# First attention of a two-block transformer kernel: split values stationary, probabilities of two token tiles moving

## The chip, the cores and the metric

The kernel runs on one core of a Trainium2 chip. The metric is the device time of one execution in microseconds (us); the kernel before takes 1032.56 us, the median of 3 runs (1032.04 to 1034.12). A lower time is better.

## The reference

One call computes two transformer blocks over 512 tokens of width 1024, all in fp32. The change concerns the attention of the first block. It has 16 heads of width 64: eight "b" heads (dilated windows, merged into one softmax with a per-distance additive term) and eight "a" heads (each token attends to the 128 keys that an indexer scores highest). Cut to what matters:

```
proj = rms_norm(x) @ w_in                  # q, k, v, z of both kinds of heads, and the indexer
for every head:
    logits = q k^T * scale + bias          # causal; 'a': only the selected keys
    p      = softmax(logits)
    o      = p v
mixed = concat(a_out * silu(za), b_out * silu(zb))
x     = x + mixed @ w_out                  # then block 2: projections, second attention, feed-forward
```

## The kernel before, in words

It is one hand-ordered program: every engine has its own list of instructions, and semaphores (wait_ge, then_inc) tie them together. Sixty-four steps make the first attention; `steps1` lists (tile i, kind, head) in groups of eight: the four token tiles of 128 tokens for the two heads r = 0, 1 of a pair, "b" first, then "a". Step t of token tile i looks at i + 1 blocks of 128 keys. The loop on every engine goes over t by two, so that one iteration has both heads of a pair at one token tile.

Large products are made in three fp32r products of a high and a low part (`three`, L869: high x high, high x low, low x high). The scores are such products (`pair1`, L1020), two heads side by side on the halves of the array. What an iteration does, by engine:

- **TensorE**: waits `l_done` for the last pair's scores to be read, then the scores of t and t + 1; the fillers of this iteration (`fill`, L869: one K chunk of a z projection at a time, 64 chunks in 56 steps, so 2 or 3 chunks of three products of 512 columns); rows of the output projection from step 58 on (`row1`, table ROW_AT); once a pair the transposes of the finished output (`mixed_transposes`, L1047); then for the steps t - 2 and t - 1 the transposes of the probabilities (`turn1`, L1029) and for t - 4 and t - 3 the value products (`value1`, L1039): per block of keys the turned probabilities, fp32, 128x128, are stationary and 64 columns of fp32 values move; the result has tokens on the partitions and collects the eight outputs of a group (both heads, four tiles) in one bank.
- **VectorE**: adds the bias to the scores and takes the row maximum in one instruction (L2164, printed as CUSTOM_DVE_ANT_0 and a read of the accumulator); copies turned probabilities out of PSUM into `probsT1` (L2177; in the second half of the steps the odd ones are ScalarE's, L1682); divides a group by its softmax denominators (`finish1`, L2120 and L2123); multiplies with silu(z) (`mix`, L2132, one operand in PSUM) and takes the low part of the mixed rows (`mixed_low`, L2146); scales the finished z tiles (`gate_rows`, L2139 and L2140); splits weight units (`low`, L1992).
- **ScalarE**: exp with the sum over the row (`exps`, L1505), silu of two z tiles at four places (L1674), the rounding of weight units (`high`, L1540), of mixed rows (L1652) and of output weights (L1669).
- **GpSimd**: from step 34 on adds the selection mask to the bias of the "a" heads (`combo`, L2612).
- **SP** issues the loads: weight units (`load_unit`, L688) into a ring of five raw and four rounded places, strips of the bias (L724, 32 transfers), parts of `w_out`.

```
pe.wait_ge(t_free, TT[("pt", u)] + 1)
for j in range(i + 1):
    last = mm(bank[6 + o % 2][:, at:at + HD], probsT1[u % 2][:, j * P:(j + 1) * P],
              v1["v" + br][:, j, h * HD:(h + 1) * HD], start=(j == 0), stop=(j == i))
```

Behind the loop comes the rest of the first row of the output projection (`first_row`), the other rows (`residual`), and the first transposes of block 2 (`h_transposes`, L918), whose input is the norm of x (L1961). The second attention, from about 513 us on, has its own code, which the change leaves alone: values split into halves that are stationary together (L1273), roundings and differences of turned probabilities (L1784, L2363), low rows (L1791, L2373), reciprocals (L2418) and scaling on GpSimd (L2664) ahead of the transposes (L1259).

## Time and profile before

| | |
|---|---|
| median of 3 runs | 1032.56 us (1032.04 to 1034.12) |
| the profiled execution | 1032.51 us |
| its span | 1030.7 us |
| TensorE busy, matmuls / weight loads | 99% / 82% |
| VectorE busy | 65% |
| ScalarE busy | 52% |
| GpSimd busy | 35% |
| granted TensorE clock, mean | 1.00 |

The span is the profiled part of the execution; 1.8 us lie around it. Busy is the share of the span in which an engine has an instruction under way; matmuls overlap in a pipeline and their ends are modelled, so that a busy TensorE may still wait. The granted clock is given as a share of full speed.

### The profile page before, as it was taken

To read this page: it belongs to the slowest core of one execution; us is meant where nothing else is said; L and a number is where in the kernel's file an instruction comes from. 1 tells how busy PE (TensorE), PEld (TensorE's weight loads), DVE (VectorE), ACT (ScalarE), POOL (GpSimd) and SP (SyncE) were. 2 spreads that over 40 slices of the span, in tenths; PEclk is the share of its full clock that TensorE was granted. 3 is DMA by queue.
4 is the path that set the end of the run, shared out by engine and by line. 5 is a ranking of instruction groups with operands and counts; after the bars stand their busy time and mean duration, and the time that the engine had idled before them with its cause. 6 is when DMAs were issued, how large, how long until landed. Compare 5 with 4: busy or idle time off the path is not lost. (4 is left out here: it accounts for less than half of the span.)

```text
span 1030.7 us, 14348 instructions
## 1 busy us (share of the span) xinstructions
PE 1019.2 (99%) x5310; PEld 843.8 (82%) x5310; DVE 665.9 (65%) x1141; ACT 534.4 (52%) x960; POOL 365.7 (35%) x334
## 2 busy tenths in 40 slices
PE   9999999999999999999999999999999999999997
PEld 7788888888878898988887788889888888888885
DVE  5578998675765346824567779444323325999996
ACT  7454445554673255545567884134434436554554
POOL 0022011003330001910165430007779965874562
PEclk9999999999999999999999999999999999999999
DMA  9655332314420285233200362239999951443552
GB/s 335 119 113 119 88 96 67 82 47 130 144 93 1 78 257 164 62 82 82 54 9 1 109 239 62 82 102 322 347 351 333 352 193 62 152 138 138 204 184 82
DMA packets 99637, 146.24 MB, mean 142 GB/s; under 512 B 6208, under 2 KB 60224, under 8 KB 99568
## 3 DMA queue, kind: packets, MB, share of 16 engines
q1 hardware_dynamic: 86016, 129.70, 38.6%
q10 hardware_dynamic: 12768, 12.88, 3.9%
q0 software_dynamic: 784, 2.75, 1.8%
q8 instruction: 42, 0.69, 0.3%
q14 instruction: 27, 0.22, 0.1%
HBM read 123.69 MB, written 21.63 MB: 141 GB/s over the span
## 5 line engine op out<-in xcount | busy, mean ns | idle before, releaser
L2462 DVE TENSOR_TENSOR w_lo<-wring,w_hi 128x1024 fp32r<-128x1024 f32 x32 | 53.0, 1658 | 105.8 <-ACT w_hi L1846 105.8
L1992 DVE TENSOR_TENSOR u_lo<-wring,u_hi 128x1024 fp32r<-128x1024 f32 (+1 forms) x64 | 80.8, 1272 | 50.9 <-ACT u_hi L1540 50.4
L869 PE MATMUL bank<-u_hi,h_hi 128*128 128x512 f32 (+1 forms) x288 | 111.0, 385 | 0.1
L869 PE MATMUL bank<-u_hi,h_lo 128*128 128x512 f32 (+1 forms) x288 | 109.4, 380 | 0.0
L869 PE MATMUL bank<-u_lo,h_hi 128*128 128x512 f32 (+1 forms) x288 | 109.1, 379 | 0.0
L1540 ACT ACTIVATE u_hi<-wring 128x1024 fp32r<-128x1024 f32 (+1 forms) x64 | 65.8, 1033 | 79.1 <-PE bank L869 57.2
L869 PE MATMUL bank<-h_hi,w_hi 128*128 128x512 f32 (+2 forms) x272 | 103.3, 380 | 0.0
L869 PE MATMUL bank<-h_hi,w_lo 128*128 128x512 f32 (+2 forms) x272 | 103.3, 380 | 0.0
L869 PE MATMUL bank<-h_lo,w_hi 128*128 128x512 f32 (+2 forms) x272 | 103.2, 380 | 0.0
L869 PE MATMUL bank<-h_hi,u_hi 128*128 128x512 f32 x224 | 94.4, 421 | 0.4 <-ACT arena L1482 0.2
L1370 PE MATMUL bank<-s_hi,f_hi 128*128 128x512 f32 x224 | 87.5, 391 | 0.7 <-DVE f_lo L2496 0.7
L869 PE MATMUL bank<-h_hi,u_lo 128*128 128x512 f32 x224 | 87.8, 392 | 0.0
L869 PE MATMUL bank<-h_lo,u_hi 128*128 128x512 f32 x224 | 87.8, 392 | 0.0
L1371 PE MATMUL bank<-s_hi,f_lo 128*128 128x512 f32 x224 | 87.4, 390 | 0.0
L1372 PE MATMUL bank<-s_lo,f_hi 128*128 128x512 f32 x224 | 87.3, 390 | 0.0
L1846 ACT ACTIVATE w_hi<-wring 128x1024 fp32r<-128x1024 f32 x32 | 33.9, 1060 | 91.9 <-PE bank L869 91.9
L2664 POOL TENSOR_SCALAR arena<-arena,stats 128x128 f32<-128x128 f32 (+3 forms) x64 | 40.4, 641 | 95.0 <-DVE stats L2418 94.9
L2488 DVE TENSOR_TENSOR s_lo<-wring,s_hi 128x2048 fp32r<-128x2048 f32 (+1 forms) x32 | 67.8, 2119 | 5.7 <-ACT s_hi L1876 5.6
L869 PEld LDWEIGHTS bank<-u_hi,h_hi 128*128 128x128 f32 x288 | 54.1, 188 | 11.5 <-issue 1.2
L2612 POOL TENSOR_TENSOR junk<-arena,x 128x256 f32<-128x256 f32 (+2 forms) x24 | 24.1, 1025 | 108.8 <-DVE stats L2164 80.3
L869 PEld LDWEIGHTS bank<-u_lo,h_hi 128*128 128x128 f32 x288 | 54.2, 188 | 10.1
L869 PEld LDWEIGHTS bank<-u_hi,h_lo 128*128 128x128 f32 x288 | 54.2, 188 | 9.4
(374 smaller groups left out, 2543.7 us busy)
## 6 DMA issues: line engine op xcount, KB each, us to landing
wring<-in_w_in SPq DMA_DIRECT2D x60, 512.0 KB, 3.9
wring<-in_w_ff ACTq DMA_DIRECT2D x12, 1024.0 KB, 8.2
wring<-sums_kept SPq DMA_DIRECT2D x16, 768.0 KB, 4.2
wring<-in_w_ff SPq DMA_DIRECT2D x22, 512.0 KB, 6.2
wring<-in_w_ff SPq DMA_DIRECT2D x32, 256.0 KB, 3.3
sums_kept<-wring SPq DMA_DIRECT2D x22, 256.0 KB, 4.9
arena<-in_w_out SPq DMA_DIRECT2D x4, 1024.0 KB, 5.1
wring<-in_w_out SPq DMA_DIRECT2D x2, 2048.0 KB, 13.5
```

The costliest lines, as they stand in the source:

```text
L869: last = mm(b, lhs, rhs, start=(start and n == 0), stop=(stop and n == 2))
L1370: mm(b, f[0][:, token], w[0][:, high], start=start, stop=False)
L1371: mm(b, f[1][:, token], w[0][:, high], start=False, stop=False)
L1372: return mm(b, f[0][:, token], w[1][:, lows], start=False, stop=stop)
L1540: run(u_hi[u % HI_UNITS][:, 0:unit_cols(u)], raw_unit(u), ACT.Copy).then_inc(u_hi_done, 1)
L1846: run(dst, src, ACT.Copy).then_inc(w_hi_done, 1)
L1992: v.tensor_tensor(u_lo[u % RAW_UNITS][:, 0:cols], raw_unit(u), u_hi[u % HI_UNITS][:, 0:cols].bitcast(F32), ALU.subtract).then_inc(u_lo_don ...
L2462: v.tensor_tensor(cut(w_lo[ring3(m)]), src, cut(w_hi[ring3(m)]).bitcast(F32), ALU.subtract).then_inc(w_lo_done, 1)
L2488: v.tensor_tensor(s_lo[pair_place(m)][:, at:PAIR], pair_raw(m)[:, at:PAIR], s_hi[m % 4][:, 0:PAIR - at].bitcast(F32), ALU.subtract)
L2612: g.tensor_tensor(combo[c % 2][:, 0:(i + 1) * P], strips[:, h, (NT - 1 - i) * P:S], mask_of[i], ALU.add)\
L2664: g.tensor_scalar(place, place, den2[:, u:u + 1], gates[:, i, at:at + 1], ALU.mult, ALU.mult).then_inc(scaled, 1)
```

## The change

The value products of the first attention take the form of the second attention's:

- Values are evicted twice (`v1_both`: rounded to the high part, and raw; GpSimd's `value_low` makes the low part), so that the high and low parts of one head's 64 columns stand side by side as one stationary operand of 128 columns.
- Turned probabilities are split too: ScalarE rounds (`turned_high`), VectorE takes the difference (`turned_low`), into places (`pt1`) in which the blocks of two token tiles lie next to each other, block j of both tiles in 256 columns. They are the moving operand. The result has the head's columns on the partitions and tokens along the row; rows 64 to 127 hold the product with the low values. `low_rows_of` (ScalarE) and `collect1` (VectorE) add them.
- `value1(o, n, r)` handles token tiles 2n and 2n + 1 of head r of pair o. For n = 0 both heads come at the iteration after the pair's last scores, for n = 1 both heads come together in the iteration t % 8 == 4.
- The probabilities are divided before they are turned: VectorE takes reciprocals of two denominators per iteration, GpSimd multiplies (`scaled`). `finish1` and the transposes of the finished output (`mixed_transposes`) go; `mix` reads the collected output from SBUF.
- Transposes stand two iterations behind the scores instead of one, and logits have eight places instead of four.
- The new operands need space: weight units of z get two raw and two rounded places (`raw_place`, `hi_place`), the strips have room for two pairs and are loaded pair by pair (`load_strips`, 48 transfers; GpSimd's `send_strip` sends four heads instead of eight), the third part of `w_out` lies elsewhere (`late_raw`), and the first units of block 2 load into places that come free with the last value product.
- Tables that set the order (LOW1, GATE_AT, WO_HIGH, ROW_AT) and the end of the loop (the last pair gated in two halves) are written for the new sequence.

```diff
+            def turned_high(u):
+                act.wait_ge(t_full, k + 1)
+                if o >= 1:
+                    act.wait_ge(pv_done, 4 * (o - 1) + 2 * (i // 2) + r + 1)
+                run(turned_place("hi", i, r), bank[4 + k % 2][:, 0:(i + 1) * P].rearrange("p (m s) -> p m s", s=P), ACT.Copy)\
+                    .then_inc(pt_hi_done, 1)
...
-            def value1(u):
-                for j in range(i + 1):
-                    last = mm(bank[6 + o % 2][:, at:at + HD], probsT1[u % 2][:, j * P:(j + 1) * P],
-                              v1["v" + br][:, j, h * HD:(h + 1) * HD], start=(j == 0), stop=(j == i))
...
+            def value1(o, n, r):
+                g, h, q, end = "v" + "ba"[o // 4], 2 * (o % 4) + r, 2 * o + n, 2 * n + 1
+                pe.wait_ge(t_free, TT[("pt", NH * o + 2 * end + r)] + 1)
...
+                both = [(j, part) for j in range(end) for part in ("hi", "lo")]
+                order = both[:-1] + [(end, "hi"), (end, "lo")] + both[-1:]
+                for j, part in order:
+                    first, cols = (0, P) if j == end else (P * (2 * (end - j) - 1), 2 * P)
+                    at = 2 * P * (r + 1) - cols
+                    last = mm(bank[6 + q % 2][:, at:at + cols], v1_both[g][j // 2][:, j % 2, h, :, :].rearrange("p m d -> p (m d)"),
+                              pt1[n, part, r][:, first:first + cols], start=((j, part) == order[0]), stop=((j, part) == order[-1]))
+                last.then_inc(pv_done, 1)
...
-                for n in range(2):
-                    if 2 <= t < NS + 2:
-                        turn1(t - 2 + n)
-                    if 4 <= t:
-                        value1(t - 4 + n)
+                if 4 <= t < NS + 4:
+                    turn1(t - 4)
+                    turn1(t - 3)
+                if t >= 8 and t % NH == 0:
+                    value1(t // NH - 1, 0, 0)
+                    value1(t // NH - 1, 0, 1)
+                if t >= 12 and t % NH == 4:
+                    value1((t - 12) // NH, 1, 0)
+                    value1((t - 12) // NH, 1, 1)
...
+                if t < NS:
+                    score1(t)
+                if 2 <= t < NS + 2:
+                    dve.wait_ge(e_done, t)
+                    v.reciprocal(den[:, t - 2:t], den[:, t - 2:t]).then_inc(rden_done, 1)
+                if t < NS:
+                    score1(t + 1)
+                if t >= 4:
+                    turned_low(t - 4)
+                    turned_low(t - 3)
+                if t >= 12 and t % NH == 4:
+                    collect1(2 * ((t - 12) // NH))
+                if t >= 16 and t % NH == 0:
+                    collect1(2 * ((t - 16) // NH) + 1)
+                    mix((t - 16) // NH)
...
+            def raw_free(u):
+                if u < F0 or u >= U2 + RAW_UNITS:
+                    return unit_free(u - RAW_UNITS)
+                if u < U2:
+                    return unit_free(u - (4 if u < F0 + 2 else 2))
+                return unit_free(U2 - 1) if u == U2 + 3 else (r_full, R_BRANCH) if u == U2 + 4 else (pv_done, VALUES)
...
+            for u in range(NS):
+                if u % 2 == 0:
+                    pool.wait_ge(rden_done, u // 2 + 1)
+                g.tensor_scalar(logits1[u % 8], logits1[u % 8], den[:, u:u + 1], None, ALU.mult).then_inc(scaled, 1)
+                if u in (9, 11, 13, 15):
+                    value_low("va", (u - 9) // 2)
+                if u + 4 in combos:
+                    combine(u + 4)
```

How the value products stand among the others on TensorE, at the end of one pair and the start of the next. Before, L1020 are scores, L869 fillers, L1029 transposes of probabilities (`consts` is the identity), L1039 value products:

```order
L1020 MATMUL bank<-qk_half 128x128 x6
L1020 MATMUL bank<-qk_half 128x256 x6
L869 MATMUL bank<-h_hi,u_hi_90 128x512
L869 MATMUL bank<-h_lo,u_hi_90 128x512
L869 MATMUL bank<-h_hi,u_lo_84 128x512
L869 MATMUL bank<-h_hi,u_hi_90 128x512
L869 MATMUL bank<-h_lo,u_hi_90 128x512
L869 MATMUL bank<-h_hi,u_lo_84 128x512
L1029 MATMUL bank<-consts,x 128x128 x4
L1039 MATMUL bank<-arena,x 128x64 x3
L1029 MATMUL bank<-consts,x 128x128 x4
L1039 MATMUL bank<-arena,consts 128x64 x3
```

And after the change, from the fillers of an iteration t % 8 == 0 on, where L930 are fillers, L1091 transposes and L1106 value products:

```order
L930 MATMUL bank<-h_hi,u_hi_89 128x512
L930 MATMUL bank<-h_lo,u_hi_89 128x512
L930 MATMUL bank<-h_hi,u_lo_82 128x512
L1091 MATMUL bank<-consts,x 128x128 x6
L1106 MATMUL bank<-pt_hi_118,vb_both_110 128x256
L1106 MATMUL bank<-pt_hi_118,vb_both_110 128x128
L1106 MATMUL bank<-pt_lo_120,vb_both_110 128x128
L1106 MATMUL bank<-pt_lo_120,vb_both_110 128x256
L1106 MATMUL bank<-pt_hi_119,vb_both_110 128x256
L1106 MATMUL bank<-pt_hi_119,vb_both_110 128x128
L1106 MATMUL bank<-pt_lo_121,vb_both_110 128x128
L1106 MATMUL bank<-pt_lo_121,vb_both_110 128x256
```

The value products have left the single steps; four matmuls of a head for the first two token tiles stand together, then four of the other head, behind the transposes.

On VectorE, what stands between the scores of two iterations where a pair begins. Before, L2164 (ISA) is the sum of scores and bias, L2132 the gating product with its operand in PSUM, L2177 copies of probabilities, L2120 and L2123 the division:

```order
L2164 ISA x,stats<-bank,arena 128x256
L2164 ISA stats 128x1
L2164 ISA x,stats<-bank,arena 128x256
L2164 ISA stats 128x1
L2132 TENSOR_TENSOR arena<-arena,bank 128x512
L2177 COPY x<-bank 128x128
L2177 COPY consts<-bank 128x128
L2120 RECIPROCAL stats<-stats 128x8
L2123 TENSOR_TENSOR arena<-bank,stats 128x512
```

After, L2263 is the sum of scores and bias, L2216 the difference of probabilities, L2224 the collecting addition, L2232 the gating product, L2271 the reciprocal:

```order
L2263 ISA x,stats<-bank,arena 128x128
L2263 ISA stats 128x1
L2216 TENSOR_TENSOR pt_lo_116<-bank,pt_hi_114 128x3x128
L2216 TENSOR_TENSOR pt_lo_117<-bank,pt_hi_115 128x3x128
L2224 TENSOR_TENSOR arena<-bank,consts 64x256 x2
L2232 TENSOR_TENSOR arena<-arena 128x512
L2263 ISA x,stats<-bank,arena 128x256
L2263 ISA stats 128x1
L2271 RECIPROCAL stats<-stats 128x2
L2263 ISA x,stats<-bank,arena 128x256
L2263 ISA stats 128x1
```

The gating product and the additions now stand between the difference that follows a transpose and the next scores.

On ScalarE from the exps of steps 12 and 13 to those of 16 and 17, after the change (L1755 rounding of probabilities, L1572 exp, L1762 low rows, L1607 a weight unit, L1746 silu):

```order
L1572 ACTIVATE x,stats<-x,stats 128x384 x2
L1607 ACTIVATE u_hi_90<-wring 128x1024
L1755 ACTIVATE pt_hi_118<-bank 128x2x128
L1755 ACTIVATE pt_hi_119<-bank 128x2x128
L1572 ACTIVATE x,stats<-x,stats 128x512 x2
L1762 ACTIVATE consts<-bank 64x512
L1746 ACT_TABLE_LOAD
L1746 ACTIVATE arena<-arena 128x512 x2
L1755 ACTIVATE pt_hi_114<-bank 128x3x128
L1755 ACTIVATE pt_hi_115<-bank 128x3x128
L1572 ACT_TABLE_LOAD
L1572 ACTIVATE x,stats<-x,stats 128x128 x2
```

The unit, asked for when its predecessor is used up, and silu with its table stand ahead of the roundings of the next iteration.

## Rows read from the trace of the kernel before

**Rows 1.** The page, part 1: busy time of the engines, share, instructions
```profile
PE 1019.2 (99%) x5310; PEld 843.8 (82%) x5310; DVE 665.9 (65%) x1141; ACT 534.4 (52%) x960; POOL 365.7 (35%) x334
```

**Rows 2.** Stages (us from:to, length, busy us and instructions, clock, DMA)
```profile
170.00:300.00 130.00, 129.10 (x914) 109.24 (x915) 84.16 (x234) 75.33 (x184) 29.62 (x28) 1.00 0.28 84
...
515.00:606.00 91.00, 89.47 (x614) 72.46 (x613) 67.38 (x225) 70.92 (x201) 49.92 (x72) 1.00 0.20 68
```

**Rows 3.** Timeline, first attention: start, us, engine, line, operation, tiles, count
```profile
203.97 0.60 PE L1047 MATMUL bank<-consts,arena 128*128 128x128 f32 x4
...
204.41 0.97 PEld L1039 LDWEIGHTS bank<-arena,x 128*128 128x128 f32 x8
...
209.52 0.30 PEld L1039 LDWEIGHTS bank<-arena,x 128*128 128x128 f32 x2
...
307.30 2.88 PE L869 MATMUL bank<-qk_half 128*128 128x512 f32 x12
```

**Rows 4.** Timeline, TensorE in the second attention and in the feed-forward
```profile
595.76 0.28 PE L1273 MATMUL bank<-pt_lo,v_both 128*128 128x256 f32 x1
...
595.88 0.28 PE L1273 MATMUL bank<-pt_hi,v_both 128*128 128x256 f32 x1
...
701.98 0.27 PE L869 MATMUL bank<-h_hi,w_lo 128*128 128x128 f32 x1
702.10 0.28 PE L869 MATMUL bank<-h_hi,w_hi 128*128 128x128 f32 x1
```

**Rows 5.** VectorE by line, 165 to 302 us: busy, mean ns, idle before
```profile
L2177 DVE COPY x<-bank 128x128 f32<-128x128 f32 (+3 forms) x32 | 15.7, 491 | 28.0 <-PE bank L1039 27.3 <-PE bank L1029 0.5
...
L2177 DVE COPY consts<-bank 128x128 f32<-128x128 f32 (+3 forms) x16 | 7.9, 491 | 4.6 <-PE bank L1039 4.5
...
L2123 DVE TENSOR_TENSOR arena<-bank,stats 128x512 f32<-128x512 f32 x8 | 5.5, 692 | 3.3 <-PE bank L1039 3.1
```

**Rows 6.** VectorE by line, whole span, second attention's instructions
```profile
L2363 DVE TENSOR_TENSOR pt_lo<-bank,pt_hi 128x128 fp32r<-128x128 f32 (+3 forms) x64 | 28.4, 486 | 19.3 <-ACT pt_hi L1784 19.1
...
L2373 DVE TENSOR_TENSOR junk<-bank,junk 64x256 f32<-64x256 f32 x16 | 6.6, 412 | 0.6 <-ACT junk L1791 0.3
...
L2418 DVE RECIPROCAL stats<-stats 128x2 f32<-128x2 f32 x32 | 5.2, 161 | 1.5 <-ACT arena L1505 1.1
```

**Rows 7.** ScalarE by line, whole span
```profile
L1540 ACT ACTIVATE u_hi<-wring 128x1024 fp32r<-128x1024 f32 (+1 forms) x64 | 65.8, 1033 | 79.1 <-PE bank L869 57.2 <-DMA wring<-in_w_in 16.2 <-DMA wring<-in_w_kwvg 5.7
...
L1784 ACT ACTIVATE pt_hi<-bank 128x128 fp32r<-128x128 f32 (+3 forms) x64 | 24.5, 435 | 22.4 <-PE bank L1259 22.2
...
L1791 ACT ACTIVATE junk<-bank 64x512 f32<-64x512 f32 x8 | 4.8, 595 | 0.2
```

**Rows 8.** GpSimd by line, whole span
```profile
L2664 POOL TENSOR_SCALAR arena<-arena,stats 128x128 f32<-128x128 f32 (+3 forms) x64 | 40.4, 641 | 95.0 <-DVE stats L2418 94.9
...
L2668 POOL TENSOR_TENSOR pm_lo<-arena,pm_hi 128x512 fp32r<-128x512 f32 x4 | 5.2, 1290 | 0.0
```

**Rows 9.** Timeline, ScalarE at its first turn to silu
```profile
196.04 0.71 ACT L1505 ACTIVATE x<-x,stats 128x512 f32<-128x512 f32 x1
...
196.85 1.28 ACT L1674 ACT_TABLE_LOAD   x1
...
199.32 1.28 ACT L1505 ACT_TABLE_LOAD   x1
```

**Rows 10.** The page, part 6: weight units, KB each, us to landing
```profile
wring<-in_w_in SPq DMA_DIRECT2D x60, 512.0 KB, 3.9
```

**Rows 11.** Timeline, GpSimd beside VectorE's difference of mixed rows
```profile
241.19 2.53 POOL L2612 TENSOR_TENSOR junk<-arena,x 128x512 f32<-128x512 f32 x2 [2.90 <-DVE stats L2164]
...
242.85 1.41 DVE L2146 TENSOR_TENSOR qk_half<-arena,qk_half 128x512 fp32r<-128x512 f32 x1
```

**Rows 12.** Timeline, input and start of the first transposes of block 2
```profile
312.68 0.75 DVE L1961 TENSOR_SCALAR arena<-x,stats 128x1024 f32<-128x1024 f32 x1
...
315.47 0.71 PE L918 MATMUL bank<-consts,arena 128*128 128x128 f32 x5
```

More of the change, by code:

```diff
@@ L541, in build @@
         strips_b_in = sem("strips_b_in")
[L542 removed]
+        strips_in = [sem(f"strips_in{n}") for n in range(2)]
+        gated_done = sem("gated_done")
         strip0_in = sem("strip0_in")
@@ L734, in _ @@
+            sp.wait_ge(a_full, AT[("za", 2)] + 1)
+            for n in range(2):
+                sp.dma_start(late_raw[n], wo[:, 2 * n:2 * n + 2, 512:D]).then_inc(wo_in[2], 16)
             for n, (name, parts) in enumerate(groups):
@@ L831, in unit_arrived @@
         def unit_arrived(eng, u):
-            eng.wait_ge(unit_in[u % RAW_UNITS], 16 * sum(len(units[m][3]) for m in range(u % RAW_UNITS, u + 1, RAW_UNITS)))
+            eng.wait_ge(unit_in[raw_place(u)], 16 * sum(len(units[m][3]) for m in range(u + 1) if raw_place(m) == raw_place(u)))
         def pair_arrived(eng, m):
@@ L1077, in _ @@
             pe.wait_ge(rel_free, IDX_HEADS * (NT - 1))
-            for t in range(0, NS + 4, 2):
+            for t in range(0, NS + 6, 2):
                 if t == HALF:
@@ L2208, in _ @@
                 norm(NT, i, xn2)
-                if i < 2:
-                    low(U2 + 2 + i)
+                if i == 0:
+                    low(U2 + 2)
             take_halves("h2", NT - 1, V_G2, h_lo)
-            for u in range(4, 11):
+            for u in range(3, 11):
                 low(U2 + u)
```

400 lines of the change are left out of this document (231 added, 169 removed).

## The prediction

> **What bounds the kernel now.** I read the page first: TensorE is busy for 99% of the span [rows 1]. Then the stages: the first attention runs from about 170 to 300 us; in these 130 us TensorE is busy for 129.1, VectorE for 84.2, ScalarE for 75.3 and GpSimd for 29.6, at a granted clock of 1.00 [rows 2]. Then the starts of single matmuls, since a busy row of a pipelined engine says little. An fp32 value product leaves two matmuls per 128x128 block, so eight for four blocks; eight of their weight loads take 0.97 us and two take 0.30, so one starts every (0.97 - 0.30) / 6 = 0.111 us. Twelve products of 512 columns take 2.88 us, which with the last one's tail of some 0.35 off is 0.23 each [rows 3]. TensorE's stream of instructions sets the time here: a matmul taken away is worth its pitch, as long as the other engines keep up. I call two steps an iteration (4.06 us now), four of them a pair of heads.
>
> **TensorE's part.** Removed: 16 heads of 10 blocks, two matmuls each: 320 x 0.111 = 35.5 us, and 32 transposes of finished outputs, (0.60 - 0.27) / 3 = 0.11 each, 3.5 us [rows 3, 4]. Added per pair of heads: 16 matmuls of 256 columns and 8 of 128. The second attention has the first form already, and one starts every 0.12 us; the form with 128 columns stands in the feed-forward, every 0.11 to 0.12 us, say 0.11 [rows 4]. That is 128 x 0.12 + 64 x 0.11 = 22.4 us. Bounds for the wide form: 0.11, and 0.15 if its moving operand, written in strips, costs extra. Net: 35.5 + 3.5 - 22.4 = **16.6 us less** (bounds 12 to 18), 2.07 us per pair.
>
> A rule speaks against the change. The Trainium skill (FP8 and Floating Point Precision, TensorE Precision Notes) says that a true fp32 product takes four passes through the array. By it the old products stream 160 x 4 x 64 = 40,960 columns and the new ones 128 x 256 + 64 x 128 = 40,960: nothing would be won but the transposes. The trace speaks otherwise: instructions of 64 columns have a pitch of 0.111 us and those of 256 one of 0.12 [rows 3, 4]; the instruction is paid for. It is rival D.
>
> **What the other engines get.** VectorE loses 48 copies of turned probabilities (15.7 + 7.9 us) and the eight divisions (5.5) [rows 5], and gets 64 differences (28.4), 32 collecting additions of 64x256 (twice the 6.6 that 16 take) and 32 reciprocals (5.2) [rows 6], and two weight units that were split before the loop, about 1.1 each: 84.2 - 29.1 + 49.0 = 104 us. ScalarE loses 16 copies, about VectorE's 7.9 for as many, and gets 64 roundings (24.5), 16 moves of the low rows (twice 4.8) and the two units (1.03 each) [rows 7]: 75.3 - 7.9 + 36.2 = 104 us. GpSimd gets 64 scalings (40.4) and 8 value differences of 1.29 [rows 8]: 29.6 + 50.7 = 80 us. TensorE's own sum is 130 - 16.6 = 113.4, so both stand at 92% of it, where the second attention, built in the new manner, has ScalarE at 70.9 and VectorE at 67.4 of 91 us with TensorE at 89.5 [rows 2]. The cover is thin.
>
> **What is late next.** All four engines now stand in one ring: scores, VectorE's sums, exp, reciprocal, GpSimd's scaling, transposes, rounding, difference, and only then VectorE's next scores, for which TensorE waits before it writes the next pair. Where ScalarE or VectorE has a burst, TensorE stalls. I price four kinds.
>
> (1) The four places where ScalarE turns to silu and back: from 196.85 to 199.32 + 1.28 = 200.60, 3.75 us [rows 9]. Before, ScalarE idles for 40% of the loop and takes it without harm. Now, at step 14, counted from TensorE's last transpose: rounding ends at 0.6, two exps at 0.8 each at 2.2 [rows 9], low rows 2.8, table and silu 5.2, two roundings 6.1; VectorE's difference 6.65, two collecting additions 7.35, the gating product 7.95, score 8.3, reciprocal 8.45, score 9.0. TensorE has till then the scores of two pairs (about 0.9, an estimate: six products side by side in twos, each at a pitch between 0.11 and 0.23), four or five weight chunks of three fillers (3.2), 14 transposes (1.5) and a value group (0.9): 6.5 us. Stall 2.5 us. The same count, with what TensorE does there, gives about 1.5, 0.5 and 2 us at steps 28, 42 and 56: 6.5 us. Bounds: 0 and 3.75 each.
>
> (2) The ring of filler weights shrinks from five raw and four rounded places to two and two, so a unit can be asked for only when its predecessor is used up. It takes 3.9 us to land [rows 10], and ScalarE, which rounds it in that same iteration, waits 1 to 2 us with its probabilities behind it, six times. Mostly long iterations cover it; at step 6 I count 1.3 us through to TensorE. Without cover it would be 8 us.
>
> (3) In the iteration that starts a pair VectorE has two differences, two collecting additions, the gating product and at times gates ahead of the scores: latency and rounding 0.75, difference 0.55, additions 0.7, product 0.6, two scores and the reciprocal 1.1, make 3.7 us of chain, against a value group 0.9, fillers 1.6 and eight transposes 0.9, 3.4 us of TensorE's work. 0.35 us for five pairs, and 0.7 more once or twice where a gate stands there: 2.4 us. Here VectorE's slow form enters: with both operands in SBUF and GpSimd at work beside it a 128x512 instruction takes 1.41 us, against 0.69 for one with an operand in PSUM [rows 5, 11]. The gating product moves to that form, and GpSimd runs nearly three times as long. For 8 gating products, 8 differences of mixed rows and 7 units at 0.5 us that is up to 11 us of VectorE's time; I let it widen the range. The Trainium skill (GPSIMD Engine Reference, the table of specifications) says that GpSimd's SBUF interfaces are shared with VectorE where that has two SBUF inputs; the trace agrees.
>
> (4) The ends. ScalarE reads each value tile twice out of PSUM, which the next group's matmuls cover but for the last tile: 0.3 us. Behind the loop the first units of block 2 load only when the probabilities' place is free, and ScalarE rounds them before it squares the first rows. Now the input of block 2's first transposes ends at 313.43 and they start at 315.47, 2 us of slack [rows 12]; I count 0.5 us lost, at most 3. The strips go out in 48 transfers instead of 32 on SP's queue, each set an iteration or more before the unit behind it is free: nothing, or some 3 us if that is wrong.
>
> Sum: -16.6 + 6.5 + 1.3 + 2.4 + 0.8 = **-5.6 us**. The profiled execution took 1032.5 us, span and what lies around it, as the median of 1032.56 does; so 1027.0.
>
> **Rivals.** A: the stalls hardly come. The second attention runs this ring in 91 / 32 = 2.84 us per iteration with TensorE busy throughout, and here an iteration has 3.5. Then most of the 16.6 stays: 1016 to 1023. Against it: no silu and little waiting for weights stands in that loop, and its engines have more room.
>
> B, slower: VectorE becomes the bound, in the iteration that starts each pair, where differences, additions and a gating product slowed by GpSimd stand ahead of the scores. Break-even: with 104 us of work VectorE must be busy for over 80% of the 130 us. If the ring holds no more than the 74 to 78% of the second attention, the loop takes 133 to 140 us: 1035 to 1042, most likely 1038. For it: the 11 us are not even in the 104. Against it: the second attention was bound by TensorE, so its share is no ceiling.
>
> C: gains and stalls cancel: 14.5 to 18.5 us of stalls, if each silu costs its full 3.75 and each pair 0.4 more. 1032.5.
>
> D: columns count, not instructions. 40,960 columns at 512 in 0.23 us are 18.4 us on both sides, the transposes give 3.5, the stalls take 11: 1040. The pitches of rows 3 and 4 speak against it.
>
> **How the numbers follow.** Forecast 0.40 (its own range 1023 to 1030), A 0.18, B 0.26, C 0.13, D 0.03. A measurement of this kernel tells 0.2%, 2.1 us, from nothing. Faster by more: forecast and A, 0.58; within: C, 0.13; slower: B and D, 0.29. The range, 1016 to 1038, holds the forecast, A, C and half of B.
>
> **What would show it.** In the profile after: value matmuls of 256 columns starting every 0.12 us; the loop at about 125 us; starts of matmuls 1 to 3 us apart just before scores behind each silu; ScalarE waiting for weight units; VectorE's gating products at 1.0 to 1.4 us. Wrong if the loop takes under 118 us (stalls overrated) or over 130 (B), if the value matmuls start 0.15 us or more apart (D), or if the loss lies behind 300 us.

## The result and the profile after

| | before | after |
|---|---|---|
| median of runs on the same chip | 1032.98 us (4 runs) | 1062.09 us (4 runs, 1059.47 to 1065.53) |
| ratio, 95% interval | | 1.0283 [1.0252, 1.0315] |
| span of the profiled execution | 1030.7 us | 1060.0 us |
| mean granted clock of TensorE | 0.999 | 0.984 |

The change costs 29 us. I had forecast 5.6 us less, with a range that ended at 1038. The page's first lines, which answer to [rows 1], and its row of the granted clock:

```profile
span 1060.0 us, 14257 instructions
...
PE 1018.4 (96%) x5150; PEld 837.0 (79%) x5150; DVE 675.5 (64%) x1207; ACT 564.7 (53%) x1033; POOL 447.2 (42%) x406
...
PEclk9999999999978999999999999999999999999999
```

TensorE is no longer busy all the time, and in the slices from 291 to 345 us the granted clock fell under 0.9. To see where the time went, I cut both traces at the same two instructions: the first score product of the first attention and the first transpose of block 2. The columns of this view are the stretch and its length, the busy time of TensorE, its weight loads, VectorE, ScalarE and GpSimd, the granted clock and the DMA's share and rate. First before, then after:

```profile
169.90:315.50 145.60, 144.60 (x982) 121.26 (x982) 96.08 (x251) 84.81 (x197) 29.62 (x28) 1.00 0.29 91
```

```profile
170.90:344.30 173.40, 143.14 (x821) 113.80 (x821) 112.89 (x319) 112.11 (x265) 107.71 (x96) 0.91 0.30 87
```

The stretch grows by 27.8 us; it starts 1.0 us later, and what follows takes 715.7 us for 715.2. So all but 1.5 of the 29.3 us lie in the loop and its end. TensorE has 160 instructions less (5310 and 5150 on the pages) and idles for 30.3 us (173.4 - 143.1) where it idled for 1.0. And its busy time hardly fell, at a clock of 0.91. What it waited for (us in total, times, longest):

```profile
PE bank L930 <- POOL qk_half L2746: 10.0, 2, 6.7
PE bank L1081 <- DVE stats L2263: 9.2, 9, 1.8
PE bank L1091 <- POOL x L2736: 5.2, 5, 1.8
PE bank L930 <- DVE arena L2242: 2.6, 1, 2.6
PE bank L930 <- DVE qk_half L2254: 2.3, 1, 2.3
PE bank L1091 <- DVE pt_lo L2216: 0.8, 1, 0.8
```

These are 30.1 of the 30.3 us. In their order: output rows (L930) that wait for GpSimd's differences of output weights; scores (L1081) that wait for VectorE to read the last ones; transposes (L1091) that wait for GpSimd's scaling; a filler that waits for VectorE to scale a finished z tile, so that its bank comes free; an output row that waits for VectorE's difference of output weights; a transpose that waits for VectorE's difference of probabilities. Cut finer in time, the second half is the worse:

```profile
230.00:260.00 30.00, 24.25 (x151) 19.49 (x149) 19.24 (x62) 18.46 (x47) 25.58 (x24) 0.94 0.62 176
260.00:290.00 30.00, 24.43 (x164) 19.22 (x163) 22.67 (x63) 24.31 (x59) 24.55 (x20) 0.99 0.18 54
290.00:320.00 30.00, 18.38 (x93) 14.52 (x92) 15.52 (x45) 17.50 (x40) 21.68 (x19) 0.78 0.05 14
```

GpSimd, 23% busy in the loop before [rows 2], is now at over 80% from 230 to 290 us. The rows of its operations there (count | busy, mean ns of one | idle before):

```profile
L2736 POOL TENSOR_SCALAR x<-x,stats 128x512 f32<-128x512 f32 x16 | 25.9, 1623 | 8.4 <-DVE stats L2271 8.4
L2736 POOL TENSOR_SCALAR x<-x,stats 128x384 f32<-128x384 f32 x16 | 20.2, 1276 | 10.5 <-DVE stats L2271 10.5
L2736 POOL TENSOR_SCALAR x<-x,stats 128x256 f32<-128x256 f32 x16 | 16.1, 1014 | 7.6 <-DVE stats L2271 7.6
L2736 POOL TENSOR_SCALAR x<-x,stats 128x128 f32<-128x128 f32 x16 | 11.6, 728 | 22.8 <-DVE stats L2271 22.8
```

That is 73.8 us, where I had taken 40.4 from the second attention's scaling [rows 8]. Same engine, same shapes, but not the same instruction: the second attention multiplies by two factors in one instruction, the new one by one. Then the end of the loop, on TensorE and on GpSimd (start, duration, operation; in brackets the idle time before and what ended it):

```profile
300.79 0.28 PE L1106 MATMUL bank<-pt_hi,va_both 128*128 128x256 f32 x1
300.91 0.28 PE L1106 MATMUL bank<-pt_lo,va_both 128*128 128x256 f32 x1
301.02 0.34 PE L1106 MATMUL bank<-pt_hi,va_both 128*128 128x256 f32 x2
...
303.27 0.60 PE L1091 MATMUL bank<-consts,x 128*128 128x128 f32 x4
310.54 1.62 PE L930 MATMUL bank<-qk_half 128*128 128x512 f32 x3 [6.66 <-POOL qk_half L2746]
...
320.70 1.19 PE L930 MATMUL bank<-za_half,qk_half 128*128 128x512 f32 x2 [3.37 <-POOL qk_half L2746]
...
323.80 0.41 PE L1106 MATMUL bank<-pt_hi,va_both 128*128 128x256 f32 x1
324.01 0.42 PE L1106 MATMUL bank<-pt_lo,va_both 128*128 128x256 f32 x1
324.23 0.42 PE L1106 MATMUL bank<-pt_hi,va_both 128*128 128x256 f32 x1
```

```profile
303.56 5.61 POOL L2736 TENSOR_SCALAR x<-x,stats 128x384 f32<-128x384 f32 x4
309.13 1.26 POOL L2746 TENSOR_TENSOR qk_half<-arena,qk_half 128x512 fp32r<-128x512 f32 x1
```

TensorE stands for 6.7 us in front of an output row (L930) that needs an output-weight difference which GpSimd only makes behind its last four scalings. The last fourteen transposes are queued behind that row, six right behind it and eight in the next iteration, so ScalarE and VectorE soon stand too; and it happens again for 3.4 us ahead of the last value products. The same three lines of value products show the other new thing: at 300.8 one starts every 0.115 us, at 323.8 every 0.215. 256 columns in 0.215 us are 1.2 per ns, the lower of the clock's two levels (1.2 and 2.4 GHz), and the granted clock there is 0.50 of full speed:

```profile
322.00:326.00 4.00, 3.94 (x15) 3.36 (x15) 0.52 (x1) 0.00 (x0) 0.23 (x1) 0.50 0.88 351
```

### The profile page after: what moved, and what is told of

Read it like the earlier page. It is cut to its first block and busy times, and to the rows that moved or that the text cites. A ratio compares the mean times of both kernels' runs of the same rounds, so it can differ in the third digit from the quotient of the medians.

```text
span 1060.0 us, 14257 instructions
## 1 busy us (share of the span) xinstructions
PE 1018.4 (96%) x5150; PEld 837.0 (79%) x5150; DVE 675.5 (64%) x1207; ACT 564.7 (53%) x1033; POOL 447.2 (42%) x406
## 5 line engine op out<-in xcount | busy, mean ns | idle before, releaser
L2570 DVE TENSOR_TENSOR w_lo<-wring,w_hi 128x1024 fp32r<-128x1024 f32 x32 | 48.0, 1499 | 110.9 <-ACT w_hi L1938 110.9
L930 PE MATMUL bank<-u_hi,h_hi 128*128 128x512 f32 (+1 forms) x288 | 111.0, 385 | 0.1
L930 PE MATMUL bank<-u_hi,h_lo 128*128 128x512 f32 (+1 forms) x288 | 109.4, 380 | 0.0
L930 PE MATMUL bank<-u_lo,h_hi 128*128 128x512 f32 (+1 forms) x288 | 109.1, 379 | 0.0
L1607 ACT ACTIVATE u_hi<-wring 128x1024 fp32r<-128x1024 f32 (+1 forms) x64 | 66.0, 1035 | 75.7 <-PE bank L930 56.4
L930 PE MATMUL bank<-h_hi,w_hi 128*128 128x512 f32 (+2 forms) x272 | 103.3, 380 | 0.0
L930 PE MATMUL bank<-h_hi,w_lo 128*128 128x512 f32 (+2 forms) x272 | 103.3, 380 | 0.0
L930 PE MATMUL bank<-h_lo,w_hi 128*128 128x512 f32 (+2 forms) x272 | 103.2, 380 | 0.0
L930 PE MATMUL bank<-h_hi,u_hi 128*128 128x512 f32 x224 | 95.2, 425 | 3.0 <-DVE arena L2242 2.6
L2736 POOL TENSOR_SCALAR x<-x,stats 128x128 f32<-128x128 f32 (+3 forms) x64 | 73.8, 1160 | 49.3 <-DVE stats L2271 49.2
L930 PE MATMUL bank<-h_hi,u_lo 128*128 128x512 f32 x224 | 89.0, 397 | 0.0
L930 PE MATMUL bank<-h_lo,u_hi 128*128 128x512 f32 x224 | 88.9, 397 | 0.0
L2791 POOL TENSOR_SCALAR arena<-arena,stats 128x128 f32<-128x128 f32 (+3 forms) x64 | 40.4, 641 | 95.0 <-DVE stats L2526 94.8
L930 PEld LDWEIGHTS bank<-u_hi,h_hi 128*128 128x128 f32 x288 | 54.1, 188 | 11.6 <-issue 1.2
L930 PEld LDWEIGHTS bank<-u_lo,h_hi 128*128 128x128 f32 x288 | 54.2, 188 | 10.1
L1968 ACT ACTIVATE s_hi<-wring 128x2048 fp32r<-128x2048 f32 (+1 forms) x32 | 54.3, 1696 | 14.1 <-PE bank L1437 14.0
```

The costliest lines, as they stand in the source:

```text
L930: last = mm(b, lhs, rhs, start=(start and n == 0), stop=(stop and n == 2))
L1607: run(u_hi[hi_place(u)][:, 0:unit_cols(u)], raw_unit(u), ACT.Copy).then_inc(u_hi_done, 1)
L1968: run(s_hi[m % 4][:, 0:PAIR - at], pair_raw(m)[:, at:PAIR], ACT.Copy).then_inc(s_hi_done, 1)
L2570: v.tensor_tensor(cut(w_lo[ring3(m)]), src, cut(w_hi[ring3(m)]).bitcast(F32), ALU.subtract).then_inc(w_lo_done, 1)
L2736: g.tensor_scalar(logits1[u % 8], logits1[u % 8], den[:, u:u + 1], None, ALU.mult).then_inc(scaled, 1)
L2791: g.tensor_scalar(place, place, den2[:, u:u + 1], gates[:, i, at:at + 1], ALU.mult, ALU.mult).then_inc(scaled, 1)
```

## The experiments

All are compared with the kernel before on the same chip; the ratio says more than the microseconds, since the runs were made at different times. In order:

**1. GpSimd's two parts.** The scaling in the second attention's form, a factor 1.0 added (e_two):

```diff
-g.tensor_scalar(logits1[u % 8], logits1[u % 8], den[:, u:u + 1], None, ALU.mult)
+g.tensor_scalar(logits1[u % 8], logits1[u % 8], den[:, u:u + 1], 1.0, ALU.mult, ALU.mult)
```

The output-weight differences 5 to 8 on VectorE, which makes all the others (e_wo):

```diff
-    WO_HIGH = {48: 0, 49: 1, 50: 2, 53: 3, 55: 4, 60: 5, 61: 6}
+    WO_HIGH = {48: 0, 49: 1, 50: 2, 53: 3, 55: 4, 60: 5, 61: 6, 63: 7}
...
-                    if WO_HIGH.get(u - 2, 5) < 5:
+                    if u - 2 in WO_HIGH:
                         wo_low(WO_HIGH[u - 2])
...
-            for m in range(5, 9):
...
```

With it ScalarE rounds the third of the four at step 63 and no longer behind the loop. Both edits are in e_two_wo; e_two_wo_nosilu has `ACT.Copy` for `ACT.Silu` besides, which leaves out the gate's nonlinearity.

> The changed kernel with one thing altered: GpSimd's 64 scalings of the probabilities multiply twice in one instruction (by the reciprocal, then by 1.0), as the second attention's do, where they now have a single operation. The result is the same. Theory G (GpSimd is late because the one-operation form takes 1.57 us for 512 columns where the two-operation form of the second attention takes 0.77): one scaling of 512 columns falls to 0.8 us or less, GpSimd's 73.8 us of scaling to about 41, its waits ahead of the transposes and the bias sums vanish, and 10 to 18 us of the 29 come back (1044 to 1052). Theory R (the ring of exp, rounding, difference and scores with silu bursts is what stalls, GpSimd's length is covered): the scalings get shorter or not, the time changes by less than 4 us. If the length comes from the place of the operands or from VectorE beside it and not from the form, it stays at 1.57 and the time at 1062.

> The changed kernel with only the end of the loop altered: the low parts of the four output-weight rows that GpSimd makes behind its last scaling are made by VectorE instead, and ScalarE rounds the third of them at step 63, as before the change. Theory Q (at the end GpSimd's queue holds the differences of the output weights behind the last scalings; TensorE stands 6.9 and 3.6 us before rows that need them, with the last transposes behind the row): both gaps close, 8 to 11 us come back (1051 to 1054). Theory R (what ends the loop is the chain of the last probabilities anyway): the gaps move to the last transposes, 0 to 3 us.

> Both alterations together: two-operation scalings and VectorE for the four differences of output weights. If they are two separate costs the gains add: 18 to 27 us, 1035 to 1044. If the end was only late because GpSimd was slow, the second adds less than 3 us to the first. By my count of the stalls that are left (silu 6.5, units 1.3, start of pairs 2.4, ends 0.8) against 16.6 us saved, it should come down to 1027; if it stays above 1036 there is a further cost that I have not named.

> As the one before, but the eight silu of the z tiles are plain copies, so that ScalarE never changes its table: silu is left out of the computation. That takes 8 table loads of 1.28 us off ScalarE. Theory S (the bursts of 3.75 us stall TensorE 0.5 to 2.5 us each, as counted): 4 to 9 us less than with silu. Theory C (they are covered): less than 2 us.

Measured: e_two 1056.74 us, 1.0235 [1.0183, 1.0288]; e_wo 1057.99, 1.0237 [1.0217, 1.0257]; e_two_wo 1049.85, 1.0168 [1.0141, 1.0194]; e_two_wo_nosilu 1045.32, 1.0116 (two runs). The two-factor form of e_two, the row that answers to the first of the four above:

```profile
L2736 POOL TENSOR_SCALAR x<-x,stats 128x512 f32<-128x512 f32 x16 | 11.0, 692 | 17.9 <-DVE stats L2271 17.9
```

0.69 us for 1.62, for the same product. Each mend brings 4 to 5 us, both together 12. The interval of e_two overlaps that of the change itself, and e_wo's just does, so only the 12 are clear of noise, and whether they are more than the sum is not shown. Both single edits fell short of their theories (10 to 18 us and 8 to 11), and the pair of its 18 to 27. The waits of the two traces show what was left: in e_two TensorE still waits 8.7 us for GpSimd's differences of output weights, in e_wo 8.4 us for the same differences on VectorE and 6.5 us for the scaling. Without the silus it is 4.5 to 5.4 us less. And 17 us above before remain, with GpSimd busy for 65 us in a loop stretch of 159.5: the further cost that the expectation of e_two_wo spoke of. GpSimd's two parts are a cause, but less than half of it.

**2. Four suspicions about the order, each alone on top of e_two_wo.** f_rows puts the first output rows later:

```diff
-    ROW_AT = {58: ((0, 0),), 60: ((0, 1),), 62: ((0, 2),), 64: ((0, 3), (0, 4)), 66: ((0, 5), (1, 0)), 68: ((1, 1), (1, 2))}
+    ROW_AT = {58: ((0, 0),), 60: ((0, 1),), 62: ((0, 2),), 66: ((0, 3), (0, 4)), 68: ((0, 5), (1, 0))}
             def first_row():
-                row1(1, 3)
+                for j in range(1, 4):
+                    row1(1, j)
```

f_gate has `HALF + 6` for `HALF + 8` in GATE_AT; f_mix calls mix() at steps of t % 8 = 2 behind the collect and not with it; f_ring moves the weight units:

```diff
-    LOW1 = {1: F0 + 1, **{filled[tile] + 2: unit_of[tile] + 2 ...
+    LOW1 = {1: F0 + 1, **{filled[tile] + 3: unit_of[tile] + 2 ...
-                    if u + 2 in LOW1:
-                        high(LOW1[u + 2])
+                    if u > 0 and u + 1 in LOW1:
+                        high(LOW1[u + 1])
```

> Base: the kernel with both mends (two-operation scaling, output-weight differences on VectorE), 1049.85 us; its trace has three gaps of TensorE at the end of the loop, 2.6 us ahead of row (0,3), 3.0 us ahead of the rows of step 68, 2.85 us ahead of the first row's tail, and granted clock 0.5 in three stretches of 3.4 us there. Edit: rows (0,3) and (0,4) go one step later (66 for 64), (0,5) and (1,0) to 68, (1,1) and (1,2) behind the last value product. Theory E (rows ahead of the last transposes make TensorE wait for output-weight and gate work and so hold up the chain transpose, split, value product): 1043 to 1047. Theory L (the chain of the last head pair through all engines sets the end, whatever stands ahead of it): 1048 to 1051, the same gaps with other names.

> Base as for f_rows. Edit: the gate of za0 stands at VectorE's step 38 for 40, so TensorE's fill of za2 (step 42) should find its PSUM bank free. Theory Z (the 2.96-us gap at 249.8 us comes from the gate's place behind collect and mix of step 40): that gap goes, 1046 to 1048. Rival: VectorE waits at the gate for the value products of head pair 3 instead and pays as much: 1049 to 1052.

> Base as for f_rows. Edit: the multiplication of gate and output (L2232) goes from VectorE's step 8o+16 to 8o+18, so that collect and mix do not stand together ahead of the next scores. Theory L (pair scores wait because one pass score, exponential, scaling, transpose, split takes longer than two steps, and VectorE's lumps lengthen it at steps with collect and mix): 1045 to 1048. Theory V (VectorE's total sets the pace, order does not matter): 1049 to 1052.

> Base as for f_rows. Edit: ScalarE's copy and VectorE's difference of each gate weight unit stand about one step (ScalarE two) later. Theory W (ScalarE stands 4 to 5 us in its queue for a weight unit whose load was only issued when its place came free, with exponentials and splits behind it): ScalarE's waits for the weight ring fall under 3 us in all and the time is 1042 to 1047. Rival (these waits lie in ScalarE's spare time, or TensorE's fill then waits for the later halves): 1049 to 1053.

Measured: f_rows 1043.63 us, 1.0100 [1.0081, 1.0119]; f_gate 1049.68, 1.0153 [1.0135, 1.0172]; f_mix 1053.73, 1.0187 [1.0164, 1.0211]; f_ring 1059.05, 1.0231 [1.0208, 1.0253]. The rows are worth 6 to 7 us, as theory E said. The other three bring nothing. f_gate came out in its rival's range and f_mix above both of its own, both with intervals that overlap e_two_wo's; f_ring came out above both, 6 us slower. f_gate's gap at the gate (of za0, the first z tile of the "a" heads: VectorE scales it, and only then its bank is free) went, but another opened close by: TensorE waits 2.5 us ahead of transposes at 257.2 for VectorE's differences, and these wait for ScalarE, which stands 5.3 us up to 254.8 in front of a weight unit. Gate and weight unit fall together, and the one had hidden the other. f_ring took ScalarE's wait for weights away altogether and still lost 6 us: the copy now stood in the step of the silus and their table loads. The two loads around the first silus stand 4.3 us apart for 3.4 in e_two_wo, and TensorE's two waits there are 1.7 and 2.6 us for 0.8 and 1.5. So ScalarE at 112 us of a 171-us stretch is not short of time, it is short of the right time.

**3. The ring of queues.** On top of f_rows: g_turn puts the transposes of a double step (an iteration) ahead of the gate's products (the fillers, which make the z tiles).

```diff
                     elif t % NH != 2:
                         pair1(t, 2)
-                    fill(fill1, t)
-                    fill(fill1, t + 1)
-                for n, j in ROW_AT.get(t, ()):
-                    row1(n, j)
                 if 4 <= t < NS + 4:
                     turn1(t - 4)
                     turn1(t - 3)
+                if t < NS:
+                    fill(fill1, t)
+                    fill(fill1, t + 1)
+                for n, j in ROW_AT.get(t, ()):
+                    row1(n, j)
```

g_nosilu is f_rows with the copies for silus, and without g_turn's edit; g_deep, on f_rows too, shifts transposes, splits, value products, collects and mix by a double step (`turn1(t - 6)`, `turned_high(t - 6)`, `turned_low(t - 6)`, and so on).

> Base: both mends and the later rows, 1043.63 us (1.0100 of before), in whose trace TensorE waits some 23 us for VectorE's scores ahead of the pair products and pays 0.9 to 3.0 us at 14 places. Edit: in each step of the loop the transposes (L1091) stand ahead of the gate's matrix products (L930) and not behind them, so that ScalarE and VectorE get them 1.5 to 2 us earlier and the products cover their time. Theory L (one pass score, exponential, scaling, transpose, split through five in-order queues is longer than the two steps the order allows it, so TensorE waits): 1034 to 1041. Rival V (the busiest engine's total sets the pace, not the order): 1042 to 1045. Rival P (TensorE now waits for the scaling ahead of the transposes, with nothing issued meanwhile): 1045 to 1055.

> Base as for g_turn. Edit: the eight silus are plain copies, so ScalarE's eight table loads and the work around them go (leaves out the gate's nonlinearity). The same edit gave 4.5 us on the kernel without the later rows. If rows and table loads are separate costs: 1037 to 1041. If the later rows had taken the same wait: 1042 to 1045.

> Base as for g_turn. Edit: transposes, their splits, value products, collects and the multiplication by the gate all stand one double step later (u-6 for u-4), so each pass has three double steps for four queues instead of two; the loop ends one double step later, and the gate of za0 stands ahead of that step's differences. Theory L: the pair products' waits for VectorE fall from 23 us under 8 us; the end costs 1 to 3 us more; 1031 to 1039. Rival V (total work of VectorE and ScalarE): 1043 to 1048.

Measured: g_turn 1039.43 us, 1.0064 [1.0051, 1.0077]; g_nosilu 1038.77, 1.0060 [1.0040, 1.0080]; g_deep 1050.35, 1.0160 [1.0147, 1.0173]. The same matmuls with the transposes first bring 4 us, within theory L's range: while TensorE does the gate's products, the other engines already have the transposes. Ahead of the scores TensorE waited 10.0 us in f_rows (by the waits view; the 23 us of the expectation are not in it) and waits 3.1 in g_turn, while its waits for VectorE's differences ahead of the transposes rise from 3.0 to 7.5. g_nosilu is 4 to 5 us under f_rows. One double step more of slack for everything (g_deep) should have brought more and cost 7 us against f_rows, above both of its ranges. In its trace TensorE waits 3.2 us at the gate of za0, 2.9 us for VectorE's scores after ScalarE has stood 7.9 us in front of a weight unit, and 4.0 us for scores once more at 284 us, ahead of which VectorE has a difference, two additions, a gating product and 2.35 us of output-weight differences. Slack between the steps doesn't help against a long wait or a lump inside one queue. That of the weight unit can be followed in g_turn's trace. SyncE's queue, then ScalarE, then TensorE:

```profile
246.36 3.59 SPq L769 DMA_DIRECT2D arena<-bias_copies  x8
249.99 0.42 SPq L734 DMA_DIRECT2D wring<-in_w_in  x1
```

```profile
249.29 0.20 ACT L1574 ACTIVATION_READ_ACCUMULATOR x<-x,stats 128x1 f32 x1
255.95 1.06 ACT L1609 ACTIVATE u_hi<-wring 128x1024 fp32r<-128x1024 f32 x1 [6.46 <-DMA wring<-in_w_in]
```

```profile
254.33 0.79 PE L1081 MATMUL bank<-qk_half 64*128 64x384 f32 x6
258.36 0.35 PE L1091 MATMUL bank<-consts,x 128*128 128x128 f32 x1 [3.25 <-DVE pt_lo L2217]
```

The unit's load is issued at 249.99, behind eight strip transfers that take 3.6 us to issue. It lands at 255.9, after 5.9 us for the median of 3.9 [rows 10], in a stretch (250 to 256 us) in which the DMA moved 239 GB/s where the whole loop has 100. ScalarE stands in front of it from 249.5 with two roundings queued behind, VectorE's differences wait for these, and TensorE's next transposes for those: 3.25 us lost at 258.36.

**4. The ring of weights, silus and GpSimd again, with the order mended.** h_ring, on top of g_turn, moves the copies away from the silus too (`filled[tile] + 5` in the diff of f_ring); h_ring_nosilu leaves out the silus; h_order is the change as made, with one-factor scaling and GpSimd's differences, and only the three edits of order.

> Base: both mends, later rows, transposes ahead of the gate's products: 1039.43 us (1.0064 of before), ScalarE idle 20.5 us in seven waits for weight units. Edit: ScalarE copies each gate weight unit 4 steps after the unit two before it is used up, VectorE takes the difference one step later still (before: 0 and 2 steps), away from the silus' step. Theory W (the wait of up to 6.5 us for a load that was only just issued holds back exponentials and splits queued behind): ScalarE's waits for the ring fall under 3 us and the time is 1034 to 1037.5. Rival (the waits lie in ScalarE's spare time): 1038.5 to 1041. If it again gets slower by 5 us or more, it is the position of the copy and not the lump with the silus.

> h_ring with the eight silus as plain copies (leaves out the gate's nonlinearity), so without the table loads. If silu is a cost of its own: 4 to 5 us under h_ring, so 1029 to 1034, and with that the first version below before. If order mends have taken up its share: 0 to 2 us under h_ring.

> The change as made (one-operation scaling and output-weight differences on GpSimd) with the three edits of order: rows later, transposes ahead of the gate's products, weight copies 4 steps later. Theory G (GpSimd's own time sets the pace of the loop's second half wherever the order puts it): 12 to 14 us over h_ring, 1047 to 1052. Theory L (the slow form cost because the order left no slack): under 6 us over h_ring, 1037 to 1043.

Measured: h_ring 1035.93 us, 1.0025 [1.0016, 1.0034]; h_ring_nosilu 1032.74, 0.9988 [0.9974, 1.0002]; h_order 1050.26, 1.0155 [1.0138, 1.0171]. Theory W stands: 3.5 to 4 us, with ScalarE's waits for weight units down from 20.5 us to 0.3. That f_ring's loss was its lump with the silus fits this, but is not shown by it alone, since h_ring also has the transposes first. The silus are worth 3 to 4 us here, between the two forecasts, and h_ring_nosilu can't be told from before. Theory G stands too: GpSimd's two parts cost 13 to 14 us with the order mended too. TensorE's waits for the scaling ahead of the transposes, in h_ring and in h_order:

```profile
PE bank L1091 <- POOL x L2738: 4.9, 6, 1.1
```

```profile
PE bank L1091 <- POOL x L2738: 14.9, 14, 2.5
```

The loop of h_ring_nosilu, cut as above:

```profile
171.20:312.90 141.70, 130.74 (x822) 103.31 (x822) 110.72 (x323) 102.90 (x257) 65.68 (x92) 1.00 0.35 107
```

In this execution the clock stays at 1.00 for the whole stretch, so its 130.7 us are what TensorE's work takes in the new form, against 144.6: **13.9 us less**. Most of that is still lost to idle time, 11 us, of which TensorE waits 5.4 us for GpSimd's scaling. It took 1030.40 us; the kernel's twelve executions took 1029.80 to 1036.14.

**5. Two last edits on h_ring.** i_split leaves one of the two gate products ahead of the transposes; i_gate puts the gate of za0 ahead of VectorE's differences of step 40; i_both has both.

> Base: the version with all mends, 1035.93 us (1.0025 of before). Edit: of the two gate products of a double step one stands ahead of the transposes and one behind. If the waits for GpSimd's scaling ahead of the transposes (0.8 to 1.3 us at six places) are what is left: 1032 to 1035. If what they cover is taken from the waits for VectorE's scores: 1035.5 to 1038.

> Base as for i_split. Edit: the gate of za0 goes ahead of the differences, the collect and the multiplication of VectorE's step 40. The gap of 0.9 us at 251.3 us goes: 1034.5 to 1035.8. Rival, as when it was put one step earlier: what stands behind it waits instead, 1036 to 1038.

> Both edits. If they add up: 1031 to 1035. If the five queues only hand the waits round: 1035.5 to 1038.

Measured: i_split 1048.10 us, 1.0134 [1.0115, 1.0153]; i_gate 1036.52, 1.0028 [1.0018, 1.0037]; i_both 1041.11, 1.0082 [1.0068, 1.0097]. i_gate is in its rival's range; the other two are above all theirs. Half a move back costs 12 us. 5 to 7 of them come from the gate of za0, by i_both's time, which with that gate mended loses only the rest. In i_both TensorE waits 6.2 us ahead of the scores where h_ring has 1.6, and 3.5 for the low parts of weight units where h_ring has 1.2. The row of i_split's waits at the gate (total, times, longest), 0.6 us in h_ring:

```profile
PE bank L930 <- DVE arena L2244: 3.7, 1, 3.7
```

No version beat before; the best, h_ring, is 0.25% slower.

## Why the prediction was wrong

The loop stretch of seven kernels, each from its own windows as above, in its one profiled execution; the surplus is its busy time less the 130.7 us at full clock, idle is length less busy; the ratio is that of all executions:

| | length | busy | surplus | idle | granted clock | ratio |
|---|---|---|---|---|---|---|
| before | 145.6 | 144.6 | | 1.0 | 1.00 | 1 |
| after | 173.4 | 143.1 | 12.4 | 30.3 | 0.91 | 1.0283 |
| e_two_wo | 159.5 | 138.5 | 7.8 | 21.0 | 0.95 | 1.0168 |
| f_rows | 154.9 | 136.0 | 5.3 | 18.9 | 0.97 | 1.0100 |
| g_turn | 150.7 | 133.6 | 2.9 | 17.1 | 0.98 | 1.0064 |
| h_ring | 147.8 | 134.3 | 3.6 | 13.5 | 0.98 | 1.0025 |
| h_ring_nosilu | 141.7 | 130.7 | 0 | 11.0 | 1.00 | 0.9988 |

Busy time times granted clock is 130 to 132 us in every row from after on, so the surplus fits what the clock took. The change's 27.8 us are thus -13.9 of TensorE's work, +29.3 of idle time and +12.4 of work at a lower clock. By the steps of the prediction:

- **TensorE's part, -16.6 (bounds 12 to 18): right, 2.7 too large.** The pitch of the new value products is 0.115 to 0.12 us at full clock. With it rival D falls: at full clock the pitch hardly changes from 64 to 256 columns (0.111 to 0.12 us), and only 512 columns take 0.23, so up to 256 it is instructions that count.
- **What the other engines get.** VectorE +16.8 us in the stretch (96.1 to 112.9) for my 20, ScalarE +27.3 for 28: right. **GpSimd's 80 us failed: 107.7.** The term "64 scalings (40.4)" was priced from a row with another instruction and measured 73.8.
- **The step that failed most was the list of stalls.** "I price four kinds", 11 us in all; 41.7 us came, 29.3 of idle time and 12.4 by the clock. Unpriced were, by what mending each brought in kernel time (which holds its share of the clock): GpSimd in the ring and at the end, 12 us (13 to 14 with the order mended); output rows in steps 64 and 66 ahead of the last transposes and in step 68 ahead of the last value products, 6 to 7; the transposes behind the gate's products, 4. Unpriced was also the gate of za0, a wait of 2.6 us. The change's list named the rows' new table, and I never asked what stands behind a row that waits.
- **(1) Silus, 6.5 us:** 3.2 to 5.4 us in three pairs of kernels, the clock's share in it. Right in kind, somewhat high. At the first silus, where I had counted 2.5 us, TensorE waits 0.79 and 1.79 us in the trace of after.
- **(2) Weight ring, 1.3 us:** ScalarE waits for four units in the trace of after, 7.4 us in all and up to 4.1, where I had six of 1 to 2. What that costs in after's own order is not known: there the one try to move the copies, f_ring, lost. With the transposes first the waits were 20.5 us, up to 6.5, and moving the copies brought 3.5 to 4. "Nothing, or some 3 us" for the strips on SyncE's queue: in g_turn eight of them stood 3.6 us in front of a load.
- **(3) Start of a pair, 2.4 us:** near in size, wrong in its causes. Ahead of the score products TensorE waits nine times for VectorE's sums, 9.2 us in all (1.6 in h_ring). Two of these waits (1.79 and 1.46 us) follow silus. Four (1.31, 1.33 and twice 0.51) end less than 1 us after VectorE itself has waited for GpSimd's mask addition, the second row below, which stands among the scalings in GpSimd's queue (with the two-factor scalings of h_ring these waits are 7.5 us too); I had GpSimd only in front of the transposes. Three are left, 2.3 us, one of them in the first pair. VectorE's slow form was not it: its gating products took 0.79 us, under the 1.0 to 1.4 I named. The first row has VectorE's waits for ScalarE's roundings, which come behind the transposes.

```profile
DVE pt_lo L2216 <- ACT pt_hi L1755: 33.2, 20, 8.4
DVE x L2263 <- POOL junk L2730: 6.8, 6, 1.7
```

- **(4) The ends, 0.8 us:** the sum is near, the places are not. The loop starts 1.0 us later, for my 0.3. Ahead of the first transposes of block 2, where I had put 0.5, TensorE does not wait; but at the loop's end it waits 2.3 us for an output-weight difference of VectorE's that I had not listed. What follows takes 0.5 us more.
- **The sign.** Rival B had the sign and neither size nor cause: VectorE is at 65% of the stretch (112.9 of 173.4), far from a bound. Rival C was also summed wrongly: silus at 3.75 each and 0.4 more per pair make 22.7 us of stalls, not 14.5 to 18.5, and so 1038.6 us. The second attention as a model, on which rival A rested, misled: its loop has no silus, gate weights, output rows or gates in the same queues.

The clock is a multiplier that I had left out. I had read 1.00 in every stretch of before and taken it as given. TensorE idled there for 1.0 us in 145.6. In the table the granted clock rises as the idle time falls, from 0.91 to 1.00, and between after and h_ring_nosilu each microsecond of idle time saved came with 0.64 more from the clock (12.4 of 19.3). Other runs lie off this order: i_split idles for 18.8 us like f_rows, with a surplus of 8.4 us for 5.3, and g_nosilu for 14.8 with 5.4. The same waits do not always lower the clock either. In h_ring TensorE waits 0.45, 0.71 and 0.64 us up to 252.2 us, and its fillers then start every 0.43 us; in h_ring_nosilu the same three waits end at 248.3, and the fillers start every 0.23. The stretches behind them, in the columns of above:

```profile
252.40:255.60 3.20, 3.20 (x9) 2.41 (x8) 2.23 (x9) 2.50 (x6) 2.40 (x4) 0.50 1.13 322
```

```profile
248.00:252.00 4.00, 3.73 (x20) 2.75 (x21) 3.27 (x13) 3.05 (x9) 2.73 (x5) 1.00 1.14 296
```

Nor does the program alone fix it: e_two took 1052.49 us at a mean clock of 0.992 and 1064.32 at 0.980. That the idle time is what lowers the clock is argued from the order in the table and from the place of the lowest stretches, behind the waits; no run changed the clock alone, and what decides between two cases like those above stays open.

What stays open: of the 11 us of idle time in h_ring_nosilu 5.4 are seven waits for GpSimd's scaling and 1.6 two waits for VectorE's sums, the rest is six waits of other kinds, and none is above 1.1 us; no run takes the scaling off GpSimd. The steps of the five groups were made on top of each other; their sizes hold in this order.

## What to carry to other kernels

Price an added instruction from a row with the same operation and the same number of operands, not just the same engine and shape; here one factor instead of two made it 2.3 times as slow. Where a change links several in-order queues into a ring, the busy share of each says little: list for each engine what stands behind every wait, and put the work that others wait for (transposes) ahead of the work nobody waits for (gate products, output rows). And where TensorE was busy all the time at full clock, count idle time at more than its face value, since the clock can fall with it (here 12.4 us beside 29.3).

## What was not expected of the hardware

- GpSimd's scaling of 128x512 by one per-row factor takes 1.62 us on average, by two factors 0.69 in the same kernel and place; 128x128: 0.73 and 0.44. The cause was not looked for; the second factor can be 1.0.
- Around TensorE's waits at the end of the loop the granted clock was 0.66 to 0.79 (in the column before the last two), with value products behind them of 256 columns at a pitch of 0.215 us instead of 0.115:

```profile
297.00:303.60 6.60, 6.60 (x39) 5.06 (x36) 3.81 (x14) 5.70 (x15) 6.35 (x8) 0.79 0.00 0
303.60:310.50 6.90, 0.27 (x3) 0.03 (x1) 2.37 (x6) 2.65 (x7) 6.78 (x6) 0.72 0.00 0
310.50:317.00 6.50, 6.46 (x33) 5.50 (x34) 2.45 (x5) 0.94 (x3) 1.25 (x1) 0.78 0.00 0
317.00:326.90 9.90, 6.47 (x26) 5.18 (x23) 4.06 (x6) 3.16 (x6) 2.86 (x2) 0.66 0.70 265
```

- Moving one instruction group within an iteration or to the next, with the same work on every engine, moved the time by 4 to 12 us in either direction (g_turn, f_ring, i_split).
